# A value table loaded in whole tiles of 1 MB instead of two halves

## The reference

```
idx = e1 * PEER_KEYS + e2              # 8 x 16 experts a token, of 128 x 128
g   = softmax(vs)
ub  = jnp.take(U, ib, axis=0)          # U: 16384 x 2048
act = gelu(einsum('thkd,td->thk', ub, xb)) * gb
vb  = jnp.take(V, ib, axis=0)          # V: 16384 x 2048
out = einsum('thk,thkd->td', act, vb)
```

## Time and profile before

| | |
|---|---|
| median of the runs | 2365.06 us |
| profiled execution | 2370.98 us, its span 2369.3 us |
| mean granted clock | 0.827 |
| busy: PE, VectorE, ACT, GpSimd | 1637.2, 1819.3, 871.3, 848.7 us |
| moved | 619.56 MB, mean 262 GB/s |
| loads of peer_v | 256 of 512 KB, 6.8 us to landing (median) |
| largest share of the chain of waits | DMA of peer_v, 15% of the span |

### The profile page before, as it was taken

How to read it: one execution, slowest core, us unless ns; L and a number is a source line. 1 busy time by engine, 2 the same in 40 slices (tenths; PEclk the granted TensorE clock), 3 DMA queues, 4 the chain that set the end, 5 groups by cost and what they waited for, 6 DMA issues and landing times. The chain is left out here.

```text
span 2369.3 us, 25309 instructions
## 1 busy us (share of the span) xinstructions
PE 1637.2 (69%) x8009; PEld 1327.3 (56%) x8009; DVE 1819.3 (77%) x2801; ACT 871.3 (37%) x1508; POOL 848.7 (36%) x586
## 2 busy tenths in 40 slices
PE   7899999898979300000122223799999999999897
PEld 6677777666979300000121122677777777777796
DVE  3298782466664899989899985788888888888666
ACT  2110003211334222212686782444444444444443
POOL 0000000000000488888777776744443444444000
PEclk9999999887989555555555556999999999999998
DMA  6324441442543799999999993499999999999363
GB/s 171 107 71 142 142 138 59 128 142 90 164 138 98 316 404 419 414 413 408 391 417 396 421 420 151 159 345 344 349 344 348 331 345 342 346 348 334 96 167 102
DMA packets 257308, 619.56 MB, mean 262 GB/s; under 512 B 28436, under 2 KB 174484, under 8 KB 215444
## 3 DMA queue, kind: packets, MB, share of 16 engines
q0 software_dynamic: 56320, 369.13, 38.7%
q1 hardware_dynamic: 200916, 249.62, 32.2%
HBM read 606.56 MB, written 12.13 MB: 261 GB/s over the span
## 5 line engine op out<-in xcount | busy, mean ns | idle before, releaser
L1124 POOL DMA_INDIRECT ring<-in_peer_u,work x128 | 125.2, 978 | 834.3 <-DVE work L1491 778.7
L1424 ACT CAST v_high<-ring 128x1024 fp32r<-128x1024 f32 x256 | 269.1, 1052 | 373.6 <-DMA ring<-in_peer_v 206.3
L1587 DVE TENSOR_TENSOR v_low<-ring,v_high 128x1024 fp32r<-128x1024 f32 x256 | 308.7, 1222 | 64.1 <-ACT v_high L1424 63.0
L262 PE MATMUL ps<-low,ring 128*128 128x288 f32 x1280 | 315.1, 410 | 7.8 <-DVE low L304 6.5
L1268 PE MATMUL ps<-v_high,act_h 128*128 128x512 f32 x896 | 296.4, 400 | 22.5 <-ACT v_high L1424 22.1
L1268 PE MATMUL ps<-v_high,act_l 128*128 128x512 f32 x896 | 291.6, 395 | 0.0
L262 PEld LDWEIGHTS ps<-low,ring 128*128 128x128 f32 x1280 | 245.6, 192 | 77.2 <-issue 8.7
L1243 PE MATMUL ps<-work 128*128 128x128 f32 x512 | 106.2, 373 | 236.3 <-ACT work L1372 215.7
L1273 PE MATMUL ps<-v_low,act_h 128*128 128x512 f32 x896 | 255.3, 401 | 13.0 <-DVE v_low L1587 12.1
L1251 PE MATMUL ps<-ident,work 128*128 128x128 f32 x6 | 1.8, 439 | 374.9 <-DVE work L1509 374.9
L1445 DVE CUSTOM_DVE_ANT_0 ring<-ring,ps 128x2048 f32<-128x2048 f32 x100 | 227.2, 2277 | 23.1 <-DMA ring<-in_peer_u,work 22.5
(11 more groups left out here) (392 smaller groups left out, 3603.8 us busy)
## 6 DMA issues: line engine op xcount, KB each, us to landing
ring<-in_peer_v SPq DMA_DIRECT2D x256, 512.0 KB, 6.8
ring<-in_w_in SPq DMA_DIRECT2D x20, 2048.0 KB, 8.2
ring<-in_w_out SPq DMA_DIRECT2D x16, 1024.0 KB, 5.8
ring<-in_w_ple_gate SPq DMA_DIRECT2D x16, 1024.0 KB, 5.8
out<-work SPq DMA_DIRECT2D x37, 256.0 KB, 3.2
work<-in_state_mlstm_C SPq DMA_DIRECT2D x32, 256.0 KB, 5.0
ring<-in_peer_w_q SPq DMA_DIRECT2D x8, 1024.0 KB, 5.6
ring<-in_w_glu SPq DMA_DIRECT2D x4, 1024.0 KB, 5.0
```

Of the source, the lines that this page charges most:

```text
L262: m = pe.matmul(ps[2 * s + c][:, 0:T], ring[:, s, k * WB + c * P:k * WB + (c + 1) * P], rhs[:, k, :], start=(k == 0), stop=(k == kt - 1))
L1124: pool.indirect_dma_start(rows[n % NR], None, u_rows, bass.IndirectOffsetOnAxis(ap=idx[:, n:n + 1], axis=0)).then_inc(sem(f"g_in{n % NR}") ...
L1424: o.do(act.copy(vh[:, hf, :], natural[b % 2][:, 1024 * hf:1024 * hf + 1024]), sem("vh_done"))
L1587: o.do(v.tensor_tensor(vl[:, hf, :], natural[b % 2][:, 1024 * hf:1024 * hf + 1024], vh[:, hf, :].bitcast(F32), ALU.subtract), sem("vl_done"))
```

## The change

Every tile of peer_v is loaded by one DMA of 1 MB, 128 pieces of 8 KB, onto `nat_row_in`. SP issues it after the second subtraction of the tile that held the slot. `nat_half_in` is gone, and with it ACT's wait for the second half. Casts, subtractions, matmuls, late rows and sample rows stay as they are.

```diff
-            def half_in(b, s, h):
-
-                sp.dma_start(natural[s][:, 1024 * h:1024 * h + 1024], b[..., 1024 * h:1024 * h + 1024]).then_inc(
-                    sem(f"nat_row_in{s}" if h == 0 else f"nat_half_in{s}"), 16)
-
             for s in range(2):
                 wait_row_read(sp, NG - 1 - (NG - 1 - s) % NR)
-                for h in range(2):
-                    half_in(v_v[:, s, :], s, h)
+                sp.dma_start(natural[s], v_v[:, s, :]).then_inc(sem(f"nat_row_in{s}"), 16)
             with sp.Fori(1, PK // 2) as i:
                 for s in range(2):
-                    for h in range(2):
-                        sp.wait_ge(sem("vl_done"), i * 4 + (2 * s + h - 3))
-                        half_in(v_v[:, ds(i * 2 + s, 1), :].rearrange("a b d -> a (b d)"), s, h)
+                    sp.wait_ge(sem("vl_done"), i * 4 + (2 * s - 2))
+                    sp.dma_start(natural[s], v_v[:, ds(i * 2 + s, 1), :].rearrange("a b d -> a (b d)")).then_inc(
+                        sem(f"nat_row_in{s}"), 16)
...
                     if hf == 0:
                         act.wait_ge(sem(f"nat_row_in{b % 2}"), 16 * (b // 2 + 2))
-                    else:
-                        act.wait_ge(sem(f"nat_half_in{b % 2}"), 16 * (b // 2 + 1))
                     if b >= 1:
                         act.wait_ge(sem("v_done"), 2 * b + hf - 1)
```

## The result

The changed kernel takes 2422.86 us, median of four runs (2415.21 to 2430.09), against 2368.82 us before (a fourth run of that kernel, 2377.78 us, moved its median from 2365.06). The ratio is 1.0223, 95% interval 1.0177 to 1.0269: 54 us slower. The direction and the range of the prediction hold; the size does not, since 26 us were forecast, less than half of it. The profiled execution is the fastest of the four, 2415.21 us for a span of 2413.5, so its trace shows 44 us of the loss. The stage took it all: from its first cast to the start of its last subtraction it was 681 us (1512.7 to 2193.8), and is 728 (1508.8 to 2236.3).

What follows compares the result with a forecast made beforehand. It took a loop through one slot (release, peer_v load, cast, subtract) to lead, no engine being full. 0.41 us over 63 turns, +26 us, on 2370.98 gave 2397; less 5.9 for the median, 2391 us, range 2335 to 2445.

Steps and rivals of the forecast that it cites:

- (c): First cast needs the whole MB: where the load leads, the one-slot loop goes from load + 2.49 to load + 3.6 us.
- (b): The first half's refill in a slot starts 1.56 us later, after the tile's second subtraction; the second half's starts as before.
- (d): peer_v loads in 8 KB pieces save 25 to 41 ns each against two of 4 KB, 0.2 to 0.33 us a tile.
- Other slots have slack: In value-stage turns not led by a load, PE ends the cast's wait and is late as before, so no growth.
- the factor 0.86: Share of turns taken as led by a load, from 88 casts of a possible 102; gives 0.41 us a turn.
- I am wrong if the chain moves to PE: Sign against the forecast: in the profile after, the chain of waits moves to PE.
- (e): Time of the 1 MB peer_v load: 8.05 us, or 7.57 once the grown turn moves it out of the gather.
- x = 0.48: Growth in us of a load-led turn of a slot, from 10.69 + x = 11.65 - x.
- The wash: Rival: the load takes 6.9 to 7.25 us, just what the longer hold costs; -12 to +10 us, chance 0.18.
- the rival with bigger pieces: 8 KB pieces pass the gather faster, load under 7.1 us; at 6.5 us -37 us, 2328 us; chance 0.25.
- No relief: Rival: the load stays at 8.05 to 9.1 us, turn 11.65 to 12.7, +60 to +127 us; chance 0.15.

Runs made afterwards that it cites:

- e2: The kernel before, but the first cast of a tile waits for both halves, refills unchanged: ratio 1.0297, +70 us.
- e10: e2 with three zero-weight matmuls of 128 columns added on PE ahead of each tile: ratio 1.0206, +49 us against the kernel before.
- e1: The kernel before, but both halves of a slot are refilled only after the tile's second subtraction: ratio 1.0043, +10 us.
- e9: The changed kernel with its one DMA of 1 MB a tile in 256 pieces of 4 KB: ratio 1.0292, +69 us against the kernel before.
- e3: The kernel before with late refill and first cast waiting for both halves, two DMAs of 512 KB: ratio 1.0321, +76 us.
- e5: The changed kernel with sample-row gathers of 256 KB instead of 1 MB: ratio 0.9987, -3 us against the kernel before.
- e6: The kernel before with each 1 MB gather split in two of 512 KB, each issued when its half buffer is free: ratio 0.9844, -37 us.

## Why the prediction was right and wrong

- **Direction and (c), load + 3.6 for load + 2.49: the right mechanism.** In the single turns of the changed kernel it is 7.50 + 3.63 = 11.13 us. Turn over 11 us: 11.44. DMA share 87%: 88%. ACT's wait for the load above 168.8 us: 208.0. That (c) alone would be 1.1 us a turn, 69 us over 63 turns, and e2 measured 70, is luck: e2's single turns did not grow at all, and about 21 of its 70 us are the half clock (e10).
- **(b) Late refill at nothing: nearly right,** +10 us (e1).
- **(d) Smaller engine time of 8 KB pieces: wrong in its reason.** The pieces saved 7 ns each, not 25 to 41, and took 355 ns against 320 to 336. What they are worth (15 to 22 us, changed kernel against e9 and e3) seems to have come mostly by the clock, which the prediction did not have.
- **The step that failed: "Other slots have slack: there PE ends the cast's wait, and PE is late next as now."** The sum let every turn grow by at most 0.48 us, and by 0.41 with the factor 0.86, and put nothing for a way through PE. For the single turns that came out: 11.13 us with a load of 7.50, where 10.69 + 0.41 and 7.57 stood. But in the other turns PE hands a late tile on. The loops of two turns grew to 23.62 us, 1.12 a turn over the mean of 10.69, with a load of 8.86 that had not become shorter; about 1 us of each such loop is PE's half clock. The 12 loops hold 27 of the 46 us in the trace, the 31 single turns 14. The mean turn grew by 0.75 us instead of 0.41.
- **The misreading behind it.** The prediction took the 9.33 us of the earlier trace rows as a piece that one cast and one subtraction follow, and all such pieces as one loop through one slot. The chain of before had 14 loops of two turns through PE beside its 24 single turns. The sign "I am wrong if the chain moves to PE" came in part: PE had 10.3% of it in the earlier trace rows and has 19.2% after (`PE ps`):

```profile
by line: DMA ring<-in_peer_v 51.5%; DVE v_low L1579 15.4%; PE ps L1262 13.0%; ACT v_high L1416 9.2%; PE ps L1267 6.2%; DVE low L1557 1.6%; issue 1.3%; DVE work L1567 0.8%; SPq L1107 0.5%; DVE act_l L1571 0.4%; DVE low L1555 0.3%; DVEq L94 0
```

- **(e) "each us of growth of the turn moves the load by as much out of the gather": the right size, and no run bears the reason out.** The load of the single turns is as short with a quarter of the gathers' bytes (7.38 in e5), so x = 0.48 came near for a reason that is not known. That is luck.
- **The rivals.** The wash and the rival with bigger pieces did not come. The latter took it that the load would pass the gather faster; its median did not move, and no run shows how the two queues share an engine. The rule of the Trainium skill ("DMA: Bandwidth & Descriptors", Rules for kernel authors) of at least 1 MiB per DMA did not decide here: one such DMA beats two of half the size only by what stands above, and halves that are cast as they land beat both. The 4.4 us that the prediction works out from the fit of that page of the Trainium skill (Anatomy of one DMA) is below every load of 1 MB here (5.1 us and more); the page gives that fit for transfers of GpSimd, and these are SyncE's. "No relief" was right for the loops of two turns, whose load of 8.86 lies in its range of 8.05 to 9.1, and wrong for the single ones.

What stays open: why the loads of the single turns take 7.4 to 7.5 us even in e5, with engines at 79%; why larger pieces go with fewer slow loops; and how the 49 and 64 us at full clock divide between the first cast's wait, the late refill and the form of the load.

## What to carry to other kernels

A transfer's size sets the step of everything behind it: if the consumer works in halves, a whole-tile load holds back the first half's work (e2: 70 us by that wait, with the half clock that it brought). The cost need not be the added time in the loop that leads; here that loop grew by 0.25 us, and most of the loss came where a late tile held up PE, which both slots share. So before counting on slack, follow the chain through the shared engine, and check each load of the chain for what really stands between it and the next. In this kernel it also paid to cut the gathers beside the stream to the size of its halves: that alone won 37 us (e6), more than any form of the load.

## What was not expected of the hardware

- PE's clock fell to 0.50 (1.2 GHz) after a stall of 3.0 us in a stage where PE was about 90% busy, and six matmuls then took 2.92 us instead of 1.40. Filling the stalls with useless matmuls made e9 21 us faster, though with them PE alone is busy for 34 us longer than the whole stage had lasted.
- 8 KB pieces of the direct load cost the engines 355 ns in this company, two of 4 KB 362 ns; the 320 ns of the gathers alone did not carry over.
- Splitting the 1 MB gathers raised the stage from 343 to 362 GB/s, with smaller pieces.
